# Loads of the chunk stage cut into half-megabyte pieces, and two expert chunks issued behind the read-out factors

## The reference

```python
u = rmsnorm(h, norm_mix[i])
proj = u @ w_in[i]
y_rw = rwkv7_mix(token_shift(proj[..., :RW_COLS], shift_mu[i]), ...)
y_gla = gla_mix(proj[..., RW_COLS:], gla_gk2[i], gla_gk_b[i], gla_norm[i])
h = h + jnp.concatenate([y_rw, y_gla], axis=-1) @ w_out[i]
u = rmsnorm(h, norm_ffn[i])
h = h + moe(u, w_router[i], b_router[i], w1[i], b1[i], w2[i], b2[i])   # 32 experts, w1 1024x2048, w2 1024x1024, f32
u = rmsnorm(h, norm_ple[i])
h = h + jax.nn.sigmoid(u @ w_ple_gate[i]) * (p[i] @ w_ple[i])
return rmsnorm(h, norm_final)
```

## Time and profile before

| what | value |
|---|---|
| runs | 1160.19, 1160.26, 1162.31 us, median 1160.26 |
| profiled execution | 1160.67 us, of which the span of its instructions is 1159.0 us |
| mean granted TensorE clock | 0.984 of full speed |
| PE busy | 1097.5 us, 95% of the span |
| DVE, ACT, POOL busy | 317.4, 217.5, 54.5 us |
| bytes moved | 432.21 MB, mean 373 GB/s |
| chain that ended last | PE 56%, DMA 40%, issue 1% |
| DMA rate by fortieths of the span | 335 206 82 52 52 286 343 357, then 426 to 431, at the end 317 and 38 GB/s |

### The profile page before, as it was taken

How to read it: one execution, slowest core, us unless ns; L and a number is a source line. 1 busy time by engine, 2 the same in 40 slices (tenths; PEclk the granted TensorE clock), 3 DMA queues, 4 the chain that set the end, 5 groups by cost and what they waited for, 6 DMA issues and landing times.

```text
span 1159.0 us, 16059 instructions
## 1 busy us (share of the span) xinstructions
PE 1097.5 (95%) x6367; PEld 492.2 (42%) x6368; DVE 317.4 (27%) x736; ACT 217.5 (19%) x397; POOL 54.5 (5%) x104
## 2 busy tenths in 40 slices
PE   8999889999999999999999999999999999999997
PEld 6876774433333333333333333333333333333334
DVE  3363454322222222222222222222222222222223
ACT  3233222211112111111111111112111111111124
POOL 8005220000000000000000000000000000000000
PEclk9999999899999999999999999999999999999999
DMA  9621178899999999999999999999999999999970
GB/s 335 206 82 52 52 286 343 357 427 426 431 428 429 429 428 429 428 429 428 428 429 429 428 429 428 430 427 429 430 429 428 429 428 428 429 428 428 428 317 38
DMA packets 42095, 432.21 MB, mean 373 GB/s; under 512 B 5364, under 2 KB 8808, under 8 KB 16936
## 3 DMA queue, kind: packets, MB, share of 16 engines
q1 hardware_dynamic: 41352, 430.10, 88.7%
q10 hardware_dynamic: 704, 1.58, 0.4%
HBM read 430.62 MB, written 1.05 MB: 372 GB/s over the span
## 4 chain that ended last, share of the span: by engine, by line
PE 56%; DMA 40%; issue 1%; POOL 1%; DVE 1%; ACT 1%; SPq 0%; DVEq 0%; POOLq 0%; ACTq 0%
PE ps L1241 52%; DMA ring<-in_w_dram 37%; DMA ring<-in_w_ple_gate_dram 2%; PE ps L1895 1%; PE ps L1822 1%; PE ps L1879 0%; DMA xb<-in_x_dram 0%; POOL xb L533 0%; PE ps L1743 0%; PE ps L1530 0%; ACT bu L662 0%; PE ps L1797 0%; SPq L318 0%; PE ps L1377 0%; POOL ring L518 0%
## 5 line engine op out<-in xcount | busy, mean ns | idle before, releaser
L1241 PE MATMUL ps<-ring,ay 128*64 128x512 f32 x1024 | 242.1, 616 | 37.2 <-DMA ring<-in_w_dram 36.2
L1241 PE MATMUL ps<-ring,gqk 128*64 128x512 f32 x1024 | 224.1, 595 | 2.8 <-DMA ring<-in_w_dram 2.6
L1156 DVE COPY t<-ps 128x512 f32<-128x512 f32 x32 | 22.1, 692 | 491.7 <-PE ps L1241 491.7
L1241 PEld LDWEIGHTS ps<-ring,ay 128*64 128x64 f32 x1024 | 72.5, 140 | 182.1 <-issue 132.6
L1241 PEld LDWEIGHTS ps<-ring,gqk 128*64 128x64 f32 x1024 | 79.0, 138 | 144.8 <-issue 140.2
L1241 PE MATMUL ps<-ring,bu 128*128 128x512 f32 (+1 forms) x240 | 88.2, 514 | 0.5 <-DMA ring<-in_w_ple_gate_dram 0.5
L766 ACT ACTIVATE t<-ps 128x512 f32<-128x512 f32 x32 | 19.1, 597 | 358.7 <-PE ps L1241 358.7
L1241 PE MATMUL ps<-bu,ring 128*128 128x256 f32 (+2 forms) x352 | 66.5, 354 | 1.2 <-DVE bu L840 1.2
L1241 PE MATMUL ps<-yb,ohgt 64*128 64x512 f32 x264 | 65.6, 615 | 0.8 <-ACT yb L781 0.8
L1241 PE MATMUL ps<-xb,oh 128*64 128x512 f32 x256 | 62.5, 607 | 0.0
L1241 PEld LDWEIGHTS ps<-bu,ring 128*128 128x128 f32 (+1 forms) x352 | 57.5, 182 | 9.9 <-DMA ring<-in_w_in_dram 1.4
(11 more groups left out here) (359 smaller groups left out, 807.3 us busy)
## 6 DMA issues: line engine op xcount, KB each, us to landing
ring<-in_w_dram SPq DMA_DIRECT2D x128, 2048.0 KB, 24.6
lg<-in_w_dram SPq DMA_DIRECT2D x16, 2048.0 KB, 26.0
bkv<-in_w_dram SPq DMA_DIRECT2D x16, 2048.0 KB, 31.3
ka<-in_w_dram SPq DMA_DIRECT2D x16, 2048.0 KB, 28.2
bu<-in_w_dram SPq DMA_DIRECT2D x16, 2048.0 KB, 29.2
ring<-in_w_in_dram SPq DMA_DIRECT2D x5, 2048.0 KB, 20.1
ring<-in_w_out_dram SPq DMA_DIRECT2D x2, 2048.0 KB, 8.7
ring<-in_w_ple_gate_dram SPq DMA_DIRECT2D x1, 4096.0 KB, 28.1
```

Of the source, the lines that this page charges most:

```text
L1156: dve.tensor_copy(HS[:, 512:1024].rearrange("p (j q) -> p j q", j=4), bank(5).rearrange("p (q j) -> p j q", j=4)).then_inc(hs1, 1)
L1241: return pe.matmul(out_, lhs, rhs, start=start, stop=stop, skip_group_check=shared)
```

## The change

`load_wout` issues its 2 MB as four loads of 128 rows by 1024 columns (512 KB, all 128 partitions), and from the second on waits until the one ahead has landed. It is called twice. The first expert chunk, `w1(0, 0, 0)`, goes in four pieces of 1024 columns in the same way, and SP then waits for the last of them. The reload of `x` becomes two loads of 512 KB, the second behind the first's landing. `load_w2(0, 0)` and `load_w1(1, 1, 0)` now stand behind the wait for `reff_ps`. The counts in the waits of DVE and PE are raised to match (`x_in` 48, `wout_in` and `wout2_in` 64, `landed_e[0]` 64); no instruction of PE, DVE, ACT or POOL is added or moved.

```diff
             def load_wout(first, s, signal):
-                sp.dma_start(slot(s, 2).rearrange("p (k n) -> p k n", k=4),
-                             w_out[0, first:first + 512, :].rearrange("(k q) n -> q k n", q=P)).then_inc(signal, 16)
+                for k in range(4):
+                    if k:
+                        sp.wait_ge(signal, 16 * k)
+                    sp.dma_start(slot(s, 2)[:, D * k:D * (k + 1)], w_out[0, first + P * k:first + P * (k + 1), :]).then_inc(signal, 16)
...
             sp.wait_ge(gg_ps, 2)
-            load_w1(0, 0, 0)
+            for n in range(4):
+                if n:
+                    sp.wait_ge(landed_e[0], 16 * n)
+                cs = slice(1024 * n, 1024 * (n + 1))
+                sp.dma_start(W1B[0][0][:, cs], w1_v[0, 0, 0][:, cs]).then_inc(landed_e[0], 16)
+            sp.wait_ge(landed_e[0], 64)
+            sp.wait_ge(wu_ps, 2)
+            for t in range(TT):
+                sp.wait_ge(x_in, 16 * (t + 1))
+                sp.dma_start(XB3[:, t, :], x[0, P * t:P * (t + 1), :]).then_inc(x_in, 16)
+            sp.wait_ge(reff_ps, 1)
             sp.wait_ge(go_ps, 2)
             load_w2(0, 0)
-            sp.wait_ge(wu_ps, 2)
-            sp.dma_start(XB3, x.rearrange("a (t q) d -> q (a t) d", q=P)).then_inc(x_in, 16)
             sp.wait_ge(y_gla, 1)
             load_w1(1, 1, 0)
-            sp.wait_ge(reff_ps, 1)
             load_w1(0, 0, 1)
...
-            dve.wait_ge(x_in, 32)
+            dve.wait_ge(x_in, 48)
...
-            pe.wait_ge(wout_in, 16)
+            pe.wait_ge(wout_in, 64)
...
-            pe.wait_ge(wout2_in, 16)
+            pe.wait_ge(wout2_in, 64)
...
-                        pe.wait_ge(on[k // 2], h * 16 + 16)
+                        pe.wait_ge(on[k // 2], h * 16 + (16 if odd or k else 64))
```

More of the change, by code:

```diff
@@ L1967, in tail @@
                 raised(0)
-                pe.wait_ge(wout_in, 32)
+                pe.wait_ge(wout_in, 80)
                 for n, (t, c, w, b) in enumerate(UNITS):
```

## The result

The changed kernel takes 1159.13 us (median of 20 runs) where the kernel before takes 1160.59 (median of 20): a ratio of 0.9982, with an interval from 0.9976 to 0.9988, so some 2 us faster. Measured once more beside two other kernels it gave 0.9982 again (0.9973 to 0.9991). One execution of the changed kernel took 2271.2 us; it is left out of the ratio, and nothing here explains it.

What follows compares the result with a forecast made beforehand. The expert weight stream at 428 GB/s was the bound, its start set by PE. PE savings 2.17 + 1.4 + 2.03 + 1.5 = 7.1 us, less 0.3 for DMA, took 1160.67 to 1153.9, median 1153.5 us; range 1152.0 to 1158.0.

Steps and rivals of the forecast that it cites:

- What bounds the kernel, and the gaps: Expert weight stream bounds; PE leaving the chunk stage sets its start; PE's 2.17 and 2.03 us gaps are late instruction fetches.
- served only when that load is nearly done, 5 to 8 us later: Chunk stage: a PE instruction fetch arriving while a 2 MB load is queued waits 5 to 8 us.
- about one block in hand: Chunk stage: PE's instruction reserve during a late fetch, a block of 256 instructions lasting some 5 us.
- The first gap, 2.17 us and the clock's 1.4: PE at 119.26 us: `w_out`'s second half in pieces removes the 2.17 us gap and the clock's fall, 1.4 us.
- the delay of the norm's rows: Group norm's rows issued at about 123.2 instead of 113.8 us, behind `w_out`'s pieces; claimed to cost nothing, covered by POOL's idle time.
- The second gap, 2.03 us and the clock's 1.5: PE at 155.74 us: `w1(0, 0, 0)` in pieces and two moved loads remove the 2.03 us gap and 1.5 us of low clock.
- Of these the DMA engines are busy 1.2 to 1.3. A fetch now waits at most that long: Chunk stage: a 0.52 MB piece takes 4.0 us to land but delays a fetch by at most 1.2 to 1.3 us.
- one gap stays: Rival near 145 us: a late fetch or a clock fall elsewhere gives back 3.6 us, 1157.1 us; chance 0.10.
- SP's waits, the cycle of 4.1 us: SP before `reff_ps`: 4.1 us per piece, second half of `x` issued by 159.8 plus 0.4, 2 us early.
- The slack of the DMA engines is used up to the last: I take 0.3 us off for it: Between `reff_ps` and the stream: 49 us of DMA work ends at 212.8 against 212.6 us, costing 0.3 us.
- The page on instruction fetch: Skill page: PE holds 2048 instructions and block crossings are mostly hidden; by it the sum of gains would be 0.

Runs made afterwards that it cites:

- the quiet kernel: Changed kernel with `w1(0, 0, 0)` and `x` loaded whole behind `reff_ps`, so no data move from 127 us to that wait; ratio 1.0038 to the kernel before.
- the kernel with the early halves: Changed kernel with half of `w_out`'s second half and half of `w1(0, 0, 0)` loaded at 77 us; ratio 0.9981 to the kernel before.

## Why the prediction was wrong

**What bounds the kernel, and the gaps.** Right. The gaps were waits for instructions: they go when the data are out of the way, at the first place with `w_out` in pieces and the norm's rows later, at the second by the moves, and the quiet kernel has neither. But "served only when that load is nearly done, 5 to 8 us later" was too long, and "about one block in hand" too much. The first fetch came at 119.0 us where it comes at 116.6 to 117.5 in the kernels without that gap, the second at 155.4 where the kernel with the moves alone has its at 152.5. A fetch that is late by 2 to 3 us stops PE for 2: it has less than one microsecond in hand.

**The first gap, 2.17 us and the clock's 1.4.** Nearly right in size: 1.7 of 2.2 us, and the clock's part whole. In its reason this is partly luck. I put the delay of the norm's rows down at "nothing"; it does cost nothing at 121.4 us, but the kernel with the early halves shows that these rows, at their old time, stop PE for 1.7 us with `w_out` out of the way. The delay that I priced at nothing may be most of the gain.

**The second gap, 2.03 us and the clock's 1.5.** This is one step that failed, at "Of these the DMA engines are busy 1.2 to 1.3. A fetch now waits at most that long" (1.3 us taken; 1.9 found here, and 2.4 in the second profile of the same kernel). I had divided a piece's bytes by the rate of a full queue. A piece alone does not reach that rate. Its landing time was right (3.6 us at 110, 4.0 at 140), but the window over the third piece of `w1` in the changed kernel shows 2.8 us of transfers at a share of 0.65, then the 1.2 us until the next one:

```profile
149.10:151.90 2.80, 1.62 (x60) 1.38 (x56) 2.42 (x6) 1.78 (x4) 1.74 (x2) 1.00 0.65 193
151.90:153.10 1.20, 1.06 (x64) 0.92 (x64) 1.20 (x2) 0.00 (x0) 0.80 (x1) 1.00 0.00 0
```

The queues tell the rest: from 144.8 to 151.4 us no instruction packet, then one, where the quiet kernel had its at 149.6:

```profile
q1 hardware_dynamic: 275, 1.03, 52.4%
...
q8 instruction: 1, 0.02, 4.9%
```

From the end of a fetch's packet to PE's going on there are 1.4 to 1.6 us at this place (151.5 + 0.9 to 154.0; before, 155.4 + 0.9 to 157.8). The fetch came 1.9 us later than in the quiet kernel, and PE stood for 1.04 us: it had 0.9 in hand, and the piece took 1.9. Nor did I see that four pieces spread over 16 us what one whole load has behind it in 6 to 8; the kernel with `w1` whole shows it. I had named this as a rival (one gap stays) and given it 0.10, though for a piece of 1.3 us. That the clock fell behind a gap of 1.04 us in one profile and not behind one of 1.21 in another was not foreseen either; in both PE had also waited 1.18 us for DVE just before. Why it fell in one and not in the other stays open.

**SP's waits, the cycle of 4.1 us.** Right: 4.0 us a cycle, the second half of `x` issued by 160.1.

**"The slack of the DMA engines is used up to the last: I take 0.3 us off for it".** The second step that failed. The sum for the engines together was near, 49 us: the middle engine is 3.0 of 3.2 us earlier at the end in this profile, 3.5 of 4.5 in the second one. But the engines are 16 queues, and the idle 3 us before the stream were also the time in which the slowest caught up. Before the change its lag is 1.3 us for the loads that land from 192 to 199 us and 0.3 at 213, in the idle time; in the changed kernel it is 2.1 from 199 to 211 and goes on into the stream. At the end it is 3.5 instead of 1.8 us, and the end moves by 1.3. The term was 1.9 us in this profile (0.3 of it the engines together, 1.6 the lag) and 2.9 in the other (1.0 and 1.9), not 0.3. Adding all of it up: 7.1 predicted on PE, 3.2 to 4.5 found; 0.3 predicted for the engines, 1.9 to 2.9 found.

**The page on instruction fetch.** The Trainium skill ("Runtime: NRT & Kernel Launch", instruction fetch mechanics) has PE hold 2048 instructions and the block change mostly hidden. The blocks of 256 agree; the reserve does not: fetches 2 to 3 us late stop PE for 1.0 to 2.2 us.

What stays open is what makes one engine the slowest. PE's own fetches (one packet of about 1 us each, on one engine) are a candidate. The kept traces speak for it without proving it: from 270 to 920 us no instruction packet is moved in the kernel before, and in no profile does the lag step there; in the kernel with only `w_out` in pieces it steps up by 0.8 between 1061 and 1071 us, and a packet of PE's instructions is moved at 1067. But elsewhere it steps down beside such a packet (in the changed kernel from 3.4 to 2.9 us at 1040), the trace has no engine numbers, and it was not tried.

## What to carry to other kernels

Judge a wait that has no releaser by the instruction packets in the trace: where the next one comes right behind a load, move that load, or make it early, rather than cut it, and look at the small loads queued behind a large one as well (here two rows of 256 KB were enough to stop PE for 1.7 us); a chain of pieces, each behind the other's landing, keeps the engines occupied for over half of its length. When a saving shortens the time ahead of a stream that is bound by DMA, look at the idle time of the engines before the stream: as it goes to zero, the saving stops arriving, and some work has to be moved out of that stretch (here half or all of `w2(0, 0)`, and the halves whose buffers were free at 77 us). The kernel with both is 0.9949 of the kernel before, the change as it was made 0.9982.

## What the runs showed of the hardware

- A load of 512 KB that is alone does not reach the rate of a full queue, at which its bytes would take 1.2 us. In the changed kernel's profile the pieces of `w_out` and `x` had packets under way for 2.1 to 2.3 us at a share near 0.8, those of `w1` for 2.6 to 2.8 at about 0.65; they landed 3.6 (at 110 us) and 4.0 us (at 140 us) after their issue.
- An instruction fetch of PE needs about 1 us (0.9 to 1.4), and PE goes on 1.3 to 1.6 us after its packet's end.
- Two loads of 256 KB in 2 KB rows, issued at 116.2 us in a profile that runs 1.8 us late, held up the fetch until 120.4, and PE stood for 1.7 us; issued at 121 to 124 us they had no gap over 0.5 us beside them.
- PE's granted clock fell to 0.50 behind waits for instructions of 2.17, 2.03 and 1.04 us, and did not behind 1.21 and 1.25 us in two other profiles.
- With no pause ahead of it, the stream keeps the lag of its start (from 280 to 915 us it changes by at most 0.02 us from load to load): one of the 16 engines is 2.3 to 4.2 us behind the middle one, where it is 1.6 to 1.8 with some 3 us of pause ahead.
